# Prompt's tile mixed last, the last latent tile's router chain between the prompt's projection passes, and the latents' ranking dealt out beside them

## The reference, cut to what matters

```
h = RMSNorm(x) * (1 + scale1) + shift1
p = h @ w_in + b_in          # q, k, v, o, gates; and u for the Fourier half
x = x + gate1 * (concat(mLSTM(q, k, v, o, gates), DFT(u)) @ w_out)
h = RMSNorm(x) * (1 + scale2) + shift2
aff = softmax(h @ router_w)                 # 16 experts
gate, idx = top_k(aff.T, 2 * n / 16)        # per expert: 128 of 1024 latents, 16 of 128 prompt rows
x[idx] += gate2 * gate * (silu(h[idx] @ w1) * (h[idx] @ w3)) @ w2
y = RMSNorm(x)
```

## Time and profile before

| | us |
|---|---|
| median of the runs | 2288.33 |
| profiled execution, its own time | 2286.71 |
| its span | 2284.6 |
| TensorE busy | 2183.0 (96% of the span) |
| VectorE busy | 499.3 (22%) |
| ScalarE busy | 353.9 (15%) |
| GpSimd busy | 261.5 (11%) |
| first expert matmul starts at | 745.13 |

### The profile page before, as it was taken

How to read it: one execution, slowest core, us unless ns; L and a number is a source line. 1 busy time by engine, 2 the same in 40 slices (tenths; PEclk the granted TensorE clock), 3 DMA queues, 4 the chain that set the end, 5 groups by cost and what they waited for, 6 DMA issues and landing times.

```text
span 2284.6 us, 37159 instructions
## 1 busy us (share of the span) xinstructions
PE 2183.0 (96%) x15091; PEld 1875.5 (82%) x15091; DVE 499.3 (22%) x1264; ACT 353.9 (15%) x1000; POOL 261.5 (11%) x263
## 2 busy tenths in 40 slices
PE   7999999999971999999999999999999999999998
PEld 2444444775640999999999999999999999999996
DVE  1111115558857111001110111111011111101113
ACT  1111112133320111111111101111011110111103
POOL 0000000102220010202102021020220201202101
PEclk9999999999995999999999999999999999999999
DMA  9720100644417659769697697986978869789692
GB/s 376 316 102 32 64 32 37 223 151 163 138 63 232 217 185 365 217 245 356 218 347 237 243 362 215 326 261 240 363 214 306 284 237 363 214 286 308 231 377 97
DMA packets 350880, 528.16 MB, mean 231 GB/s; under 512 B 12916, under 2 KB 291564, under 8 KB 347512
## 3 DMA queue, kind: packets, MB, share of 16 engines
q1 hardware_dynamic: 336456, 509.35, 64.4%
q0 software_dynamic: 14384, 18.29, 3.7%
HBM read 492.23 MB, written 35.36 MB: 231 GB/s over the span
## 4 chain that ended last, share of the span: by engine, by line
PE 66%; DVE 1%; POOL 0%; issue 0%; ACT 0%; DMA 0%; DVEq 0%; ACTq 0%; POOLq 0%
PE ps_pair L1731 44%; PE ps_pair L1744 22%; DVE ring L1886 0%; DVE ring L1881 0%; PE ps_pair L1764 0%; POOL xe L1641 0%; DMA xe_p<-normed,slot_row_p 0%; ACT squares L1711 0%; PE ps_pair L1758 0%; DVE xeS L1810 0%; DVE xeT L1818 0%; PE ps_pair L1769 0%; PE ps_pair L1779 0%; POOL rs L1664 0%; ACT rs L1713 0%
## 5 line engine op out<-in xcount | busy, mean ns | idle before, releaser
L1731 PE MATMUL ps_pair<-xeT,ring 128*128 128x144 f32 x8192 | 1008.6, 286 | 14.7 <-DVE xeT L1821 14.7
L1731 PEld LDWEIGHTS ps_pair<-xeT,ring 128*128 128x128 f32 x8192 | 1006.9, 190 | 14.8 <-issue 14.8
L1744 PE MATMUL ps_pair<-hidT,ring 128*128 128x144 f32 x4096 | 504.4, 286 | 0.0
L1744 PEld LDWEIGHTS ps_pair<-hidT,ring 128*128 128x128 f32 x4096 | 502.8, 190 | 0.0
L465 PE MATMUL ps_p<-w_in_sb,hT 128*128 128x512 f32 x720 | 318.8, 596 | 3.0 <-DMA w_in_sb<-in_w_in 3.0
L1825 DVE TENSOR_TENSOR hidT<-silu,ps_pair 128x144 f32<-128x144 f32 x256 | 77.9, 304 | 883.6 <-ACT silu L1680 883.6
L465 PEld LDWEIGHTS ps_p<-w_in_sb,hT 128*128 128x128 f32 x720 | 134.5, 191 | 158.0 <-issue 156.9
L1655 POOL DMA_INDIRECT stream<-ye,slot_row x60 | 94.7, 1579 | 1135.2 <-DVE ye_p L1836 1121.5
L1680 ACT ACTIVATE silu<-ps_pair 128x144 f32<-128x144 f32 x256 | 74.5, 291 | 909.2 <-PE ps_pair L1731 909.2
L1162 PE MATMUL b_z<-y,shared 128*128 128x512 f32 x288 | 128.0, 597 | 4.1 <-DVE soft L1384 3.5
L1829 DVE STREAM_TRANSPOSE yS<-yT 128x1024 f32<-128x1024 f32 x15 | 18.7, 1245 | 425.9 <-ACT yT_p L1687 425.9
(11 more groups left out here) (286 smaller groups left out, 1063.6 us busy)
## 6 DMA issues: line engine op xcount, KB each, us to landing
ring<-in_exp_w SPq DMA_DIRECT2D x384, 1024.0 KB, 12.4
y<-in_ada_w SPq DMA_DIRECT2D x22, 1024.0 KB, 8.1
w_in_sb<-in_w_in SPq DMA_DIRECT2D x4, 2048.0 KB, 21.5
shared<-kvo SPq DMA_DIRECT2D x15, 512.0 KB, 5.7
kvo<-pr SPq DMA_DIRECT2D x9, 768.0 KB, 3.3
qkT_dram<-qkT SPq DMA_DIRECT2D x9, 512.0 KB, 4.7
qk<-qkT_dram SPq DMA_DIRECT2D x9, 512.0 KB, 5.6
m_in<-m_lanes SPq DMA_DIRECT2D x9, 512.0 KB, 6.1
```

The source lines that it names most:

```text
L1731: mm = nc.tensor.matmul(ps_ab[f % 2][:, N * w:N * w + N], unit[:, k, bass.ts(c, P)], xeT[:, k], start=(k == 0), stop=(k == DT - 1))
L1744: mm = nc.tensor.matmul(ps_yy[d % 2][:, 0:N], unit[:, f % 2, bass.ts(d, P)], hT[:, f], start=(f == 0), stop=(f == FT - 1))
```

## The change

Turn n now handles tile (n + 1) mod 9, so the latents come first and the prompt last. The loops of turns are written out. Turns 0 to 8 keep their order on each engine. From turn 9 on each engine has a list of its own: turn 9 turns the heads ahead of the rows, and the rows go to `b_n`; the prompt's projection (`last`) is cut into pieces of one to seven blocks, and between them stand the router sums, logits' and affinities' transposes of latent tiles 7 and 8, which use `b_i` and `b_n`. The prompt's own router chain comes behind it. VectorE's ranking of the latents (`sort_steps`, 48 steps: largest, strike, places, sixteen times) is taken out of the routing block and put into the mixing block, dealt out between the residual of the prompt and its router chain; the prompt's ranking (`sort_prompt`) and the rest of the latents' follow at the end of the mixing block. The ranking's buffers lie in the latents' gate row, which is free after their last residual. In the routing block the order of the transposes and of one copy changes. SP's list in the routing block is not changed. All loads and stores of the mixing block go by tile(n).

```diff
+    def tile(n):
+        return (n + 1) % TILES
+    def group(n):
+        return 0 if tile(n) == 0 else 1
...
-    def turns(engine, steps, turn, per=None):
-        for i in range(5):
-            turn(i, i % 2, i // 2)
-        with (engine.Fori(0, 2) if steps is None else steps.loop(engine, 2, per)) as j:
-            turn(j * 2 + 5, 1, j + 2)
-            turn(j * 2 + 6, 0, j + 3)
-        for i in range(9, TILES + 4):
-            turn(i, i % 2, i // 2)
...
+    for i in range(TILES):
+        turn(i, i % 2, i // 2)
+    soften(TILES)
+    square(TILES, 1, 0)
+    keep_heads(TILES, 1)
+    square(TILES, 1, 1)
+    keep_rows(TILES, b_n, range(4, DT))
+    soften(TILES + 1)
+    keep_rows(TILES + 1, b_n, range(4, DT))
+    soften(TILES + 2)
+    square(TILES + 1, 0, 0)
+    square(TILES + 1, 0, 1)
+    keep_rows(TILES + 2, b_n, range(DT))
+    soften(TILES + 3)
...
+    def project(i, par, h, blocks=range(DT)):
+        if blocks[0] == 0:
+            pe.wait_ge(mix_act, i - 1)
+            pe.wait_ge(mix_pool, i - 1)
+            if not below(i, 3):
+                pe.wait_ge(out_kept, 2 * i + (h - 5))
+        for k in blocks:
             mm = nc.tensor.matmul(b_z[h][:], mixT[:, par, k], g.w_out_sb[:, k, bass.ts(h, 512)], start=(k == 0), stop=(k == DT - 1))
-        mm.then_inc(out_summed, 1)
+        if blocks[-1] == DT - 1:
+            mm.then_inc(out_summed, 1)
     def prompt_sum():
...
+    def turn_rows(i, banks):
         pe.wait_ge(xn2_ready, i - 2)
-        if on(i, 2):
+        if below(i, TILES):
             pe.wait_ge(out_kept, 2 * i - 2)
-        elif on(i, 4):
-            pe.wait_ge(negmax_ready, i - 3)
+        else:
+            pe.wait_ge(comb_done, 2 * TILES)
         for k in range(DT):
-            mm = nc.tensor.transpose(b_z[k // 4][:, bass.ts(k % 4, P)], xn2[:, bass.ts(k, P)], g.ident)
+            mm = nc.tensor.transpose(banks[k // 4][:, bass.ts(k % 4, P)], xn2[:, bass.ts(k, P)], g.ident)
         mm.then_inc(x2_turned, 1)
...
+    def route(i, bank):
+        pe.wait_ge(h2T_dve, min(i - 3, TILES - 1))
         pe.wait_ge(h2T_act, i - 3)
+        pe.wait_ge(inter_kept, 2 * min(i, TILES))
         for k in range(DT):
             j = k % 4
-            mm = nc.tensor.matmul(ps_logits[32 * j:32 * j + 2 * E], router[:, k], h2T[:, k], start=(k < 4), stop=(k >= 4))
+            mm = nc.tensor.matmul(bank[32 * j:32 * j + 2 * E, 0:P], router[:, k], h2T[:, k], start=(k < 4), stop=(k >= 4))
         mm.then_inc(logits_summed, 1)
...
-    turns(pe, None, turn)
+            turn_heads(i)
+    for i in range(TILES):
+        turn(i, i % 2, i // 2)
+    before_last, last = TILES, TILES + 1
+    route(before_last, b_z[1])
+    project(before_last, 1, 0)
+    turn_logits(before_last, b_z[1])
+    pe.wait_ge(negmax_ready, before_last - 3)
+    project(before_last, 1, 1)
+    turn_aff(before_last)
+    turn_heads(before_last)
+    turn_rows(before_last, b_n)
+    project(last, 0, 0, range(0, 3))
+    route(last, b_i[0])
+    project(last, 0, 0, range(3, 4))
+    turn_logits(last, b_i[1])
+    turn_rows(last, b_n)
+    project(last, 0, 0, range(4, 6))
+    turn_aff(last)
+    route(last + 1, b_i[0])
+    project(last, 0, 0, range(6, 7))
+    turn_logits(last + 1, b_i[1])
+    project(last, 0, 0, range(7, 8))
+    project(last, 0, 1, range(0, 1))
+    turn_aff(last + 1)
+    project(last, 0, 1, range(1, DT))
+    turn_rows(last + 1, b_n)
+    route(last + 2, b_i[0])
+    turn_logits(last + 2, b_i[1])
+    turn_aff(last + 2)
...
+    def sort_steps(first, last):
+        for n in range(first, last):
+            r, step = divmod(n, 3)
+            eight = slice(8 * r, 8 * r + 8)
+            rows, struck = (g.aff_rows[:, PROMPT:], g.sort_rows)[::-1 if r % 2 else 1]
+            if step == 0:
+                settle(sorted_by.get("struck"))
+                did(nc.vector.max(g.top[:, eight], rows))
+                sorted_by["top"] = g.dve.mark()
+            elif step == 1:
+                settle(sorted_by["top"])
+                if r < CAP_L // 8 - 1:
+                    did(nc.vector.match_replace(struck, g.top[:, eight], rows, -1.0))
+                    sorted_by["struck"] = g.dve.mark()
+            else:
+                did(nc.vector.max_index(g.at[:, eight], g.top[:, eight], rows))
...
+    for i in range(TILES):
+        turn(i, i % 2, i // 2)
+    before_last, last = TILES, TILES + 1
+    keep_logits(before_last, b_z[1])
+    outputs(before_last, 1, before_last // 2)
+    even_rows(before_last, 1)
+    residual(before_last, 1, before_last // 2, 0)
+    soften(before_last)
+    residual(before_last, 1, before_last // 2, 1)
+    keep_aff(before_last)
+    keep_rows(before_last, b_n[0])
+    even_rows(last, 0)
+    keep_logits(last, b_i[0])
+    largest(last, b_i[1])
+    soften(last)
+    keep_rows(last, b_n[0])
+    keep_aff(last)
+    keep_logits(last + 1, b_i[0])
+    largest(last + 1, b_i[1])
+    soften(last + 1)
+    keep_aff(last + 1)
+    settle()
+    residual(last, 0, last // 2, 0)
+    sort_steps(0, 9)
+    residual(last, 0, last // 2, 1)
+    sort_steps(9, 12)
+    even_rows(last + 1, 1)
+    sort_steps(12, 19)
+    keep_logits(last + 2, b_i[0])
+    sort_steps(19, 20)
+    largest(last + 2, b_i[1])
+    sort_steps(20, 21)
+    soften(last + 2)
+    sort_steps(21, 22)
+    keep_aff(last + 2)
+    sort_prompt()
+    sort_steps(22, 3 * (CAP_L // 8))
     settle()
...
     @block.tensor
     def _(pe):
         ident = g.ident[0:E, 0:E]
-        pe.wait_ge(picked, 1)
-        nc.tensor.transpose(ps[1][0:CAP_P, 0:E], top_p[:], ident)
-        nc.tensor.transpose(ps[1][0:CAP_P, E:2 * E], at_pf[:], ident).then_inc(slots_turned, 1)
-        pe.wait_ge(picked, 2)
-        nc.tensor.matmul(ps[1][:, bass.ts(1, 2 * E)], g.spread_slots[0:CAP_P, :], prompt_slots[:], start=True, stop=True).then_inc(slots_turned, 1)
-        pe.wait_ge(picked, 6)
+        nc.tensor.transpose(ps[1][0:CAP_P, 0:E], top_p, ident)
+        nc.tensor.transpose(ps[1][0:CAP_P, E:2 * E], at_pf, ident).then_inc(slots_turned, 1)
+        pe.wait_ge(picked, 4)
         for n in range(4):
             for c in range(4):
                 mm = nc.tensor.transpose(ps[0][:, 4 * E * n + E * c:4 * E * n + E * c + E], spread[n][:, c].rearrange("e q r -> e (q r)"), ident)
         mm.then_inc(slots_turned, 1)
+        pe.wait_ge(picked, 5)
+        nc.tensor.matmul(ps[1][:, bass.ts(1, 2 * E)], g.spread_slots[0:CAP_P, :], prompt_slots[:], start=True, stop=True).then_inc(slots_turned, 1)
     @block.vector
     def _(dve):
         did, settle = g.dve.did, g.dve.settle
...
-    def pick(src, spare, values, places, n):
-        for r in range(n // 8):
-            eight = slice(8 * r, 8 * r + 8)
-            did(nc.vector.max(values[:, eight], src))
-            settle()
-            if r < n // 8 - 1:
-                did(nc.vector.match_replace(spare, values[:, eight], src, -1.0))
-            struck_out = g.dve.mark()
-            did(nc.vector.max_index(places[:, eight], values[:, eight], src))
-            settle(struck_out)
-            src, spare = spare, src
-    pick(g.aff_rows[0:E, 0:PROMPT], spare[0:E, 0:PROMPT], top_p, at_p, CAP_P)
-    settle()
-    did(COPY(at_pf[:], at_p[:]), picked)
-    pick(g.aff_rows[:, PROMPT:], spare[:], top, at, CAP_L)
-    dve.wait_ge(slots_turned, 1)
-    did(COPY(prompt_slots[:], ps[1][0:CAP_P, 0:2 * E]), picked)
-    settle()
     def fourfold(x):
...
     did(nc.vector.tensor_scalar(spread[3][:], fourfold(at[SECOND:HALVES, ::-1]), float(PROMPT + LATENT // 2), None, ALU.add), picked)
-    dve.wait_ge(slots_turned, 3)
+    dve.wait_ge(slots_turned, 1)
+    did(COPY(prompt_slots[:], ps[1][0:CAP_P, 0:2 * E]), picked)
+    dve.wait_ge(slots_turned, 2)
     L4 = 4 * E
     did(COPY(gate_b[:], ps[0][:, 2 * L4:3 * L4]))
     did(COPY(row_b[:], ps[0][:, 3 * L4:4 * L4]))
...
+    at = sb("at", [HALVES, CAP_L + CAP_P], dt=U32)
+    g.at, g.at_p = at[:, 0:CAP_L], at[0:E, CAP_L:]
+    picks = g.gate1[:, 1]
+    g.top, g.top_p, g.at_pf = picks[0:HALVES, 0:P], picks[0:E, P:P + CAP_P], picks[0:E, P + CAP_P:P + 2 * CAP_P]
+    g.sort_rows, g.sort_rows_p = picks[0:HALVES, D // 2:], picks[0:E, 2 * P:3 * P]
```

More of the change, by code:

```diff
@@ L919, in turn @@
                         sp.wait_ge(xn2_q_ready, i - 2)
-                        sp.dma_start(g.normed[bass.ts(i - 3, P), :], xn2_q).then_inc(normed_stored, 16)
+                        sp.dma_start(g.normed[bass.ts(tile(i - 3), P), :], xn2_q).then_inc(normed_stored, 16)
                     if on(i, 2):
                         sp.wait_ge(x2_ready, 2 * i - 2)
-                        sp.dma_start(g.stream[bass.ts(i - 2, P), :], x2[:, par]).then_inc(stream_stored[par], 16)
+                        sp.dma_start(g.stream[bass.ts(tile(i - 2), P), :], x2[:, par]).then_inc(stream_stored[par], 16)
                         if on(i, 0):
                             load_x(i, par)
[L927 to L932, removed]
+                for i in range(TILES + 3):
```

(34 more changed lines are left out.)

164 lines of the change are left out of this document (85 added, 79 removed).

## The result

| | median, us | runs | ratio to before, 95% |
|---|---|---|---|
| before | 2288.35 | 2287.78 to 2290.04 | |
| changed | 2298.11 | 2296.58 to 2299.18 | 1.0042 [1.0032, 1.0053] |
| predicted | 2300.0 | 2294 to 2306 | |

What follows compares the result with a forecast made beforehand. Everything from the first expert matmul was taken as a fixed 1539.5 us; ahead of it SP's start +20.0, less slack 9.2, plus 0.9, gave +11.7: 2298.4 profiled, plus 1.6 for the median, 2300.0; range 2294 to 2306.

Steps and rivals of the forecast that it cites:

- The last arrival: End of the routing block: SP's twelve load issues, starting 712.7 and ending 743.5, come last; VectorE stands 25 us; chance 0.81.
- faster rival: End of the routing block: SP is not last if twelve issues take under 19.1 us; -10.8 us, 2277.5; chance 0.10.
- no change: Routing block: SP's issues shorten in part, to 17 to 22 us; the time lands within 0.2%; chance 0.04.
- Order and loops: Mixing block's turns: tile 0 last costs nothing, written-out loops give -0.6 us, bounds -0.9 and +2.
- The prompt's projection: Last projection in the mixing block: starts 2.65 us earlier, at 658.4, takes 3.4 us of inserted pieces, ends at 676.3.
- TensorE's stall: Between the last projection's passes: TensorE waits 0.8 us because VectorE's even rows of tile 8 meet POOL's copy.
- The dealt-out ranking: VectorE's list in the mixing block from 670.6: 40.5 us of work plus waits; ranking ends at 712.2, bounds 709.5 and 715.
- The wait for the prompt's router sum: VectorE's list after ranking step 18: a gap of 1.4 us until ScalarE's row blocks and TensorE's sum are done.
- The gathers beside the rest of the traffic: First expert's gathers meet the last 6.9 us of weight traffic: +0.7 us, bounds 0 and +3.2.

## Why the prediction was right, and which terms were off

**The last arrival.** Right. SP's first issue was forecast for 712.7, the last for 743.5, VectorE idle for 25 us; the trace has 713.03, 743.86 and 25.34. That the first two meet to 0.4 us is luck: the ranking was taken 1.25 us too long, and in this trace turn 9 starts 1.6 us later than forecast. The wait itself doesn't hang on either. Four loads instead of twelve take the loss away and more; the same edit in the kernel before makes it slower. The faster rival (SP not last) fell with 30.83 us for twelve issues, against the 19.1 at which it would have decided, and "no change" (17 to 22 us) with it. It was right as a picture of another kernel: with four loads ahead of the block's end its 2277.5 was forecast and 2276.2 measured.

Behind the faster rival the prediction put what the Trainium skill states in "DMA: Bandwidth & Descriptors", section "Anatomy of one DMA": many descriptors can be emitted before the cost of emitting shows. That section describes transfers that GpSimd issues, and these loads are SP's, so it speaks neither for nor against. Here four of SP's issues took 6.69 us, less than their transfer of some 12 us, and each further one some 3.0.

**Order and loops.** Forecast -0.6, measured from turn 4's to turn 8's score matmul, compare:

```profile
534.68 1.06 PE L1148 MATMUL b_s<-qk 128*128 128x128 f32 x8
...
619.10 1.06 PE L1148 MATMUL b_s<-qk 128*128 128x128 f32 x8
```

84.42 us against 85.03: -0.61. But this sum is one turn short: turn 8 stood in the loop too, and from its score matmul to turn 9's transpose of affinities it is 38.20 us for 38.46, another -0.26. The loops are worth -0.87, not -0.6. Longer code showed no price.

**The prompt's projection.** Its rows, for the earlier trace rows:

```profile
659.24 2.84 PE L1176 MATMUL b_z<-y,shared 128*128 128x512 f32 x6 [0.36 <-ACT shared L1060]
...
661.23 2.48 DVE L1448 TENSOR_SCALAR shared<-shared,ss 128x1024 f32<-128x1024 f32 x1 [0.61 <-POOL ss L965]
661.28 1.89 POOL L972 TENSOR_TENSOR y_prompt<-shared,ss 128x1024 f32<-128x1024 f32 x1
...
663.97 0.33 PE L1241 MATMUL b_i<-const,gate_rows 128*128 128x128 f32 x1 [0.26 <-DVE gate_rows L1441]
...
670.47 6.17 PE L1176 MATMUL b_z<-y,shared 128*128 128x512 f32 x14
...
689.49 1.08 PE L1235 MATMUL b_i<-shared,router 128*32 128x128 f32 x16 [3.04 <-issue]
```

Turn 9 starts 0.99 us later than before in this trace. With that taken off the projection starts at 658.25 (forecast 658.4) and ends at 675.65 (676.3). TensorE's stall was mis-sized: the logits' transpose at 663.97 waited 0.26 us, forecast 0.8. The sum has a slip besides: its terms (676.0 - 2.65 + 3.4 - 0.8 + 0.8) give 676.75, not 676.3. The inserted pieces took some 3.0 us instead of 3.4, which hides it. None of this is on the path, for VectorE takes both residual halves without a wait.

VectorE did meet POOL's copy both times, 2.48 us as taken. Which of the two came first the rows leave open: VectorE's start is recorded 0.05 us ahead of POOL's (661.23, 661.28), and yet POOL's copy lasts its usual 1.89 and VectorE ends 0.54 us behind it. Only the run with a wait that puts VectorE first shows that order decides (0.75 us).

**The dealt-out ranking.** Its end lies 55.24 us behind the start of the stretch, forecast 56.5: 1.25 too long: the last latent affinities were kept at 669.96 (turn 9's 0.99 taken off; 670.6 forecast), and VectorE's list from there took 41.6 us instead of 42.2. The wait for the prompt's router sum came at the forecast place with 1.52 us (1.4).

**The gathers beside the rest of the traffic.** Mis-sized. I took +0.7 out of 0 to 3.2; the last landing took 4.13 us for 2.54, and from POOL's first instruction of the block to the matmul it is 13.67 us for 12.16: +1.5. The upper bound of 3.2 was right: 3.14 and 3.18 us where the traffic is full.

**The sum.** Ranking -1.25, gathers +0.8: the stretch is 100.64 where 101.1 was forecast (88.82 + 11.7 + 0.6). The profiled execution took 2299.05 us (forecast 2298.4), because its turn 4 started 1.86 us later than in the trace before (534.68 for 532.82), which lies within what identical code shows. The median is 1.9 below the forecast; 0.5 of that is the stretch, 0.3 the loops and 0.3 what lies behind the first matmul. The rest, 0.8, comes from adding 1.6 for the distance between a profiled execution and its median, which one execution doesn't fix: for the changed kernel the distance was -0.9. By the traces the change costs 11.8 - 0.9 - 0.3 = 10.6 us, the medians show 9.8 and 9.9, and the 0.8 us between them are inside the intervals.

## What to carry to other kernels

Work that is moved over the end of a block takes with it everything that stands behind that end on every other queue; price the queue that had slack (here 9.2 us) before the engine that gains (14 us). Put long rows of loads where they start early, hold only as many of them ahead of a common end as pass before the engine that is last there (eight here), and keep the rest away from the small transfers that the next stage waits for. Read a gain from inside the stretch, and see whether the median confirms it.

## What the runs showed of the hardware

- SP's issues of plain loads of 1 MB are short only at first: the first two of the changed kernel took 1.01 us together; 4, 8 and 12 in a row took 6.69, 18.62 to 18.91, and 30.43 to 30.84 us. Beyond the fourth each takes 3.0 us, the time of its own transfer at 348 GB/s. An estimate from this: some two loads (12 us of transfer less 6.69) are taken ahead of their transfer.
- The end of a block waits for issues, not for bytes: the engines left 0.4 us after SP's last issue, with 349 GB/s still moving.
- A row of five gathers costs 3.1 to 3.2 us more under full weight traffic (5.7 to 5.8 us for the last landing) than alone (2.5); behind all twelve loads, beside their last bytes, the last landing took 4.1 to 4.5.
- VectorE's operation on 128x1024 elements takes 0.75 us alone and 2.48 to 2.49 where it meets POOL's copy of 1.89 to 1.90; a wait that puts VectorE first brings the 0.75 back.
- A longer idle time of TensorE cost no more than the time itself: at a granted clock of 0.50 (1.2 GHz) before the first expert in every trace, its first half took 65.06 and 65.04 us after 40.7 and 40.6 us of idleness, and 64.39 to 65.93 after 14.3 to 30.4.
- Identical code starts turn 9 up to 3.4 us apart in two executions (655.29 and 658.68), while the stretch behind it repeats within 0.1 us (74.30 and 74.31).
